# The last head's keys turned by DMA, its level products in pairs, an evacuation spread over chunks, and the front's modulation chunks four in a run

## The reference, cut to what matters

```
mod = silu(c) @ w_ada + b_ada;  shift, scale, gate = split(mod, 3)
h = rms_norm(x, norm_w) * (1 + scale) + shift
rq, rk, rv, rg, hq, hf_f, hf_b, hi, hg = split(h @ w_in, 9)
# HGRN2, in chunks: b = cumsum(log f)
scores = einsum(q, k, exp(b_i - b_j), causal)
o = scores @ v + (q * exp(b)) @ s
s = exp(b_last) * s + (k * exp(b_last - b)).T @ v
out = concat(o_r, o_h) @ w_out;  y = rms_norm(x + gate * out)
```

## Time and profile before

| | us |
|---|---|
| median of 3 runs | 1402.6 (1402.54 to 1402.9) |
| the profiled execution | 1402.41 |
| its span, first to last instruction | 1400.6 |
| TensorE busy | 1383.0 (99%) |
| VectorE busy | 1000.2 (71%) |
| ScalarE busy | 483.8 (35%) |
| GpSimd busy | 368.6 (26%) |
| mean granted TensorE clock | 0.999 of full |

### The profile page before, as it was taken

How to read it: one execution, slowest core, us unless ns; L and a number is a source line. 1 busy time by engine, 2 the same in 40 slices (tenths; PEclk the granted TensorE clock), 3 DMA queues, 4 the chain that set the end, 5 groups by cost and what they waited for, 6 DMA issues and landing times.

```text
span 1400.6 us, 24706 instructions
## 1 busy us (share of the span) xinstructions
PE 1383.0 (99%) x10042; PEld 1165.1 (83%) x10042; DVE 1000.2 (71%) x1330; ACT 483.8 (35%) x842; POOL 368.6 (26%) x292
## 2 busy tenths in 40 slices
PE   7999999999999999999999999999999999999997
PEld 5788898889888988898889888988898888888886
DVE  5555676667689888988888888877676768532345
ACT  4323243234333433342334333333333344221234
POOL 0000114311532153215321532153206225201220
PEclk9999999999999999999999999999999999999999
DMA  9994342434354535454444454433433358183235
GB/s 387 418 418 162 117 126 68 121 73 138 89 165 113 169 101 169 110 156 119 161 116 140 128 155 125 131 97 106 113 99 87 103 149 280 52 305 96 90 106 210
DMA packets 207735, 212.40 MB, mean 152 GB/s; under 512 B 144256, under 2 KB 156816, under 8 KB 202768
## 3 DMA queue, kind: packets, MB, share of 16 engines
q1 hardware_dynamic: 207600, 210.89, 48.0%
q10 hardware_dynamic: 32, 0.02, 0.0%
HBM read 182.27 MB, written 24.40 MB: 148 GB/s over the span
## 4 chain that ended last, share of the span: by engine, by line
PE 95%; DMA 3%; DVE 1%; SPq 0%; issue 0%; ACT 0%; DVEq 0%; ACTq 0%
PE ps L2133 10%; PE ps L2135 10%; PE ps L2134 10%; PE ps L1968 9%; PE ps L1969 8%; PE ps L1970 8%; PE ps L1944 8%; PE ps L2317 5%; PE ps L2319 5%; PE ps L2318 5%; DMA area<-in_w_mod 2%; PE ps L2150 2%; PE ps L1975 2%; PE ps L1976 2%; PE ps L1977 2%; PE ps L1934 2%
## 5 line engine op out<-in xcount | busy, mean ns | idle before, releaser
L1202 DVE TENSOR_TENSOR w_lo<-area,w_hi 128x1024 fp32r<-128x1024 f32 x143 | 190.4, 1331 | 206.3 <-ACT w_hi L730 206.3
L730 ACT ACTIVATE w_hi<-area 128x1024 fp32r<-128x1024 f32 x143 | 151.5, 1059 | 482.3 <-PE ps L2135 257.6
L2133 PE MATMUL ps<-w_hi,hT_hi 128*128 128x512 f32 x640 | 250.5, 391 | 0.0
L2135 PE MATMUL ps<-w_hi,hT_lo 128*128 128x512 f32 x640 | 249.1, 389 | 0.0
L2134 PE MATMUL ps<-w_lo,hT_hi 128*128 128x512 f32 x640 | 249.0, 389 | 0.0
L1968 PE MATMUL ps<-hT_hi,w_hi 128*128 128x512 f32 x512 | 204.8, 400 | 0.0
L1969 PE MATMUL ps<-hT_lo,w_hi 128*128 128x512 f32 x512 | 199.7, 390 | 0.0
L1970 PE MATMUL ps<-hT_hi,w_lo 128*128 128x512 f32 x512 | 199.6, 390 | 0.0
L2135 PEld LDWEIGHTS ps<-w_hi,hT_lo 128*128 128x128 f32 x640 | 120.1, 188 | 25.0
L2133 PEld LDWEIGHTS ps<-w_hi,hT_hi 128*128 128x128 f32 x640 | 120.2, 188 | 24.6
L2134 PEld LDWEIGHTS ps<-w_lo,hT_hi 128*128 128x128 f32 x640 | 120.2, 188 | 24.6
(11 more groups left out here) (282 smaller groups left out, 2426.5 us busy)
## 6 DMA issues: line engine op xcount, KB each, us to landing
area<-in_w_in SPq DMA_DIRECT2D x144, 512.0 KB, 4.3
area<-in_w_mod SPq DMA_DIRECT2D x26, 1024.0 KB, 12.3
area<-in_w_out SPq DMA_DIRECT2D x38, 512.0 KB, 3.8
gate_raw<-in_w_gate SPq DMA_DIRECT2D x32, 512.0 KB, 3.8
gate_raw<-in_w_mod SPq DMA_DIRECT2D x6, 1024.0 KB, 12.1
o_hi_scratch<-area SPq DMA_DIRECT2D x56, 80.0 KB, 2.4
o_lo_scratch<-area SPq DMA_DIRECT2D x56, 80.0 KB, 2.4
hT_hi<-o_hi_scratch SPq DMA_DIRECT2D x14, 320.0 KB, 7.2
```

What stands on the lines that cost most here:

```text
L730: act.activation(split_weights(h, n)[0], raw[:, n % 3, :], ACT.Copy).then_inc(wt_hi.sem, 1)
L1202: v.tensor_tensor(lo, raw[:, n % 3, :], hi.bitcast(F32), ALU.subtract).then_inc(wt_lo.sem, 1)
L2133: mm(out, hT_hi[:, k, tile_cols(t)], w_hi[:, n % 2, w], start=k == 0, stop=False)
L2135: i = mm(out, hT_lo[:, k, tile_cols(t)], w_hi[:, n % 2, w], start=False, stop=k == KT - 1)
```

## The change

It has four parts. (1) The last head's keys go the way of the other heads: `turn_keys` on DVE, `move_keys` on SP (behind `load_w_out(2)`); PE's eight transposes and ACT's two copies go, and `chunk_updates` waits for the DMA. (2) On PE, levels 4 and 5 of the last head's products stand together behind `first_block(3, 1)`, and 6 and 7 together behind `first_block(5, 0)`; products 5 and 7 get banks of their own; `place(4)` and `place(6)` now wait until both products of their pair are done. On DVE, `own_decay(5)` moves behind `differences(6)` and `place(6)` behind `own_decay(6)`. (3) In the last output block, DVE's evacuation of tiles 2, 3 and 4 is spread over three chunks. (4) In the front's four periods from e = 3 on, all four modulation chunks run together behind `first_group(e, 0)` and the queries.

```diff
 def ctx_scores(following, product):
     if following is None:
-        return ps[:, BB if product <= 2 else DD, 0:P]
+        return ps[:, BB if product <= 2 else DD, 0:P] if product not in (5, 7) else ps[:, DD, P:2 * P]
 def scores_bank(following, product):
-    return C if following is not None and product in (5, 7) else A
+    return C if product in (5, 7) else A
@@ sync
     load_w_out(2)
+    move_keys(last)
     store_states(last, n_ret_f, n_ret_b, rst, r_state, r_state_stored)
@@ scalar: keys() and its call go
     decays(last, 2)
-    keys(last)
     split_w(2)
@@ vector
 def place(h, following, product):
-    scored, placed = pe_level.at(h, (product if following is None else product | 1) + 1), h_sT.at(h, product)
+    scored = pe_level.at(h, (product if following is None and product < 4 else product | 1) + 1)
+    placed = h_sT.at(h, product)
...
     tokens_last(h)
-    if not isinstance(h, int) or h < HEADS - 1:
-        turn_keys(h)
+    turn_keys(h)
...
     place(last, None, 4)
     differences(last, 5)
-    own_decay(last, 5)
     place(last, None, 5)
     differences(last, 6)
-    place(last, None, 6)
+    own_decay(last, 5)
     split_w(5)
     own_decay(last, 6)
+    place(last, None, 6)
     hgrn_silu(last, 2)
     split_w(6)
     hgrn_silu(last, 3)
     place(last, None, 7)
...
+    late = nb == OUT_BLOCKS - 1
     if j == 2:
-        finish(nb - 1, 2, TILES)
+        finish(nb - 1, 2, 3 if late else TILES)
+    if late and j in (3, 4):
+        finish(nb - 1, j, j + 1)
@@ tensor
 for e in range(3, WCHUNKS - 1):
-    c0 = (e + 1) * GROUP_CHUNKS
-    ada_chunk(c0)
-    ada_chunk(c0 + 1)
     first_group(e, 0)
     first_queries(0, range(e + 1, e + 2))
-    ada_chunk(c0 + 2)
-    ada_chunk(c0 + 3)
+    for c_ in range((e + 1) * GROUP_CHUNKS, (e + 2) * GROUP_CHUNKS):
+        ada_chunk(c_)
     first_group(e, 1, range(0, 1))
...
 def chunk_updates(h):
-    if h == HEADS - 1:
-        pe.wait_ge(last_keys.sem, last_keys.at(0))
-    else:
-        pe.wait_ge(k_moved.sem, k_moved.at(h))
-        pe.wait_ge(r_S.sem, r_S.at(h))
-        pe.wait_ge(r_state.sem, r_state.at(h))
+    pe.wait_ge(k_moved.sem, k_moved.at(h))
+    pe.wait_ge(r_S.sem, r_S.at(h))
+    pe.wait_ge(r_state.sem, r_state.at(h))
...
-    if following is None or product in (2, 4, 6):
+    if product in (2, 4, 6) or following is None and product in (1, 3):
         pe.wait_ge(h_sT.sem, h_sT.at(h, product))
...
-    pe.wait_ge(r_scaled.sem, r_scaled.at(last))
-    key_tokens(last)
     pe.wait_ge(h_sT.sem, h_sT.at(last, 3))
     for kk in range(WK):
         first_block(0, kk, shared)
+    pe.wait_ge(r_scaled.sem, r_scaled.at(last))
     chunk_updates(last)
...
     first_block(3, 0)
+    first_block(3, 1)
     level_scores(last, None, 4)
-    first_block(3, 1)
     level_scores(last, None, 5)
     first_block(4, 0)
-    level_scores(last, None, 6)
     first_block(4, 1)
     first_block(5, 0)
+    level_scores(last, None, 6)
     level_scores(last, None, 7)
     first_block(5, 1)
     hgrn_outputs(last)
```

More of the change, by code:

```diff
@@ L325, in layer @@
         h_sq, h_rms, h_gated = Signal("h_sq"), Signal("h_rms", 2), Signal("h_gated")
-        last_keys, pe_hu, pe_level = Signal("last_keys", 2), Signal("pe_hu"), Signal("pe_level", PRODUCTS)
+        pe_hu, pe_level = Signal("pe_hu"), Signal("pe_level", PRODUCTS)
         pe_ho = Signal("pe_ho")
@@ L858, in retention_norm @@
                 i.then_inc(r_scaled.sem, 1)
[L860 to L864, removed]
             def context_states(h):
@@ L2201, in retention_columns, with chunk_updates @@
                 nc.tensor.transpose(ctx_columns(following), sT[:, 0:P], ident).then_inc(pe_columns.sem, 1)
-            def key_tokens(h):
-                pe.wait_ge(h_kl.sem, h_kl.at(h))
+            def chunk_updates(h):
+                pe.wait_ge(k_moved.sem, k_moved.at(h))
                 pe.wait_ge(r_S.sem, r_S.at(h))
                 pe.wait_ge(r_state.sem, r_state.at(h))
[L2208 to L2214, removed]
-                if h == HEADS - 1:
-                    pe.wait_ge(last_keys.sem, last_keys.at(0))
-                else:
-                    pe.wait_ge(k_moved.sem, k_moved.at(h))
-                    pe.wait_ge(r_S.sem, r_S.at(h))
-                    pe.wait_ge(r_state.sem, r_state.at(h))
                 for i, t in enumerate((0, 1, 2, 3)):
```

## The result

The kernel after takes 1406.67 us (median of 8 runs, 1406.02 to 1408.48), the kernel before 1402.65 (8 runs, 1402.33 to 1403.91) on the same chip: a ratio of 1.0029, 95% interval 1.0020 to 1.0038. That is slower by 4.0 us, where +1.6 was predicted, and outside the range of 1401.8 to 1406.2. The profiled execution of after took 1407.79 us, so it is one of the longer ones; its span grew by 5.4 us, from 1400.6 to 1406.0.

The account below looks back on a forecast made before the run. TensorE, busy for 99% of the span, was taken to bound the kernel. The terms -0.2 - 0.9 + 1.4 + 0.2 - 0.6 + 2.3 - 0.6 gave +1.6 us, median 1402.6 to 1404.2, range 1401.8 to 1406.2.

Parts of the forecast that it names:

- Levels 4 and 5: Last head: VectorE waits about 4 us at place(4), but three half blocks (10 us) precede level 6, so no cost.
- `place(7)`, +2.3: Last head: TensorE waits at hgrn_outputs for VectorE's place(7), delayed by work queued behind place(6); +2.3 us, bounds 2.0 and 2.6.
- Two pairs, -0.6: Last head's level products: running levels in pairs saves one pair of run ends, 0.28 us each, -0.6 us for two.
- -0.9, +1.4 and +0.2: Last head's keys: transposes gone -0.9 us; TensorE waits for VectorE's late retention_chain +1.4; follow-up at split_w(2) and state chain +0.2.
- Front, -0.2: Front's four periods: runs of four chunks save 1.28 us, waits for the low half cost 0.5 + 3 x 0.2; -0.2 us.
- The upper bound: Front: +0.5 us if each restart costs twice the forecast amount.
- Evacuations, -0.6: Last output block: the 0.34 us wait for a split behind three evacuated tiles goes, with overlap and restart; -0.6 us.
- the rivals: VectorE keeps up, 1399.2 us (6%); keys come late, 1407.2 (7%); front's slots run dry, 1406.2 to 1407.4 (10%).
- "Slower": Whole kernel: a time above 1405.4 us, from the two slow rivals and the forecast's edge; 19%.
- the keys or the slots: Slow rivals: last head's keys landing 3 us late, 1407.2 us (7%); front's chunk refills late, 1406.2 to 1407.4 us (10%).

Follow-up runs that it names:

- e1: The kernel before with only the paired level products (TensorE's and VectorE's order, two new buffers); 1407.06 us.
- e3: The kernel after with VectorE's hgrn_silu(2) moved ahead of own_decay(6) and place(7) put directly behind place(6); 1403.83 us.
- e4: The kernel after with levels 6 and 7 apart again, TensorE's order, banks and waits as before for them; 1404.88 us.
- e8: The kernel of e3 with levels 4 and 5 apart again as before, 6 and 7 still paired; 1402.24 us.
- e12: The kernel before with three reciprocals and a 32-column copy, read by nobody, added on VectorE ahead of hgrn_silu(3); 1407.96 us.
- e13: The kernel of e8 with the last head's keys on TensorE and the front as before; 1401.28 us.
- e6: The kernel before with only the spread evacuations of the last output block; 1401.61 us.
- e2: The kernel before with only the last head's keys turned by VectorE and moved by DMA; 1403.29 us.
- e5: The kernel before with only the front's run of four modulation chunks; 1402.34 us.
- e11: The kernel before with two reciprocals and a 128-column copy, read by nobody, added on VectorE ahead of hgrn_silu(3); 1404.59 us.
- e9: The kernel of e7 with SP's queue reordered: o loads ahead of move_keys, state stores and load_w_out(3) between its write and reads; 1403.70 us.
- e10: The kernel of e8 with the keys turned behind retention_chain and SP's order as in e9; 1402.76 us.
- e7: The kernel of e2 with VectorE's turn_keys moved behind retention_chain; 1404.20 us.

## Why the prediction was wrong

By medians the parts alone give +0.2 (front), +1.0 (keys), -0.6 (evacuations), and the pairs +3.3 without and about +4.8 with the fall of the clock. Without it the sum is +3.8 (unrounded); the five shorter runs of after lie 3.7 over before (1406.37 to 1402.65), the three longer ones 5.1 or more. So the parts add up. Of the miss of 2.4 us, 1.6 lie in the pairs (+3.3, where -0.6 + 2.3 was forecast), and what is left in the keys (0.3) and the front (0.4), each of them within the noise.

- *"Levels 4 and 5: VectorE waits about 4 us at `place(4)`, but three half blocks (10 us) follow before level 6. Nothing."* This step failed. It held VectorE's wait against TensorE's next product and stopped there. It did not ask what VectorE hands on behind `place(4)`, namely `differences(5)`, without which ScalarE's `decays(5)` and then GpSimd's `key_decay(5)` cannot start, nor did it name GpSimd's own `differences(5)`, for which the end of product 4 frees a buffer. Put off by 3.2 us, the chain for levels 5 and 6 (differences, exponentials, products) ends after TensorE has come to level 7. It showed as 1.1 us ahead of level 7 (after, e1, e3), as 2.3 ahead of level 6 when that was moved up (e4), and as nothing when product 4 went back (e8).
- *`place(7)`, +2.3.* Right in place, releaser and nearly in size: 2.09. e3 confirms the reason: it came from three operations of VectorE queued between `place(6)` and `place(7)`, and it goes when one of them is put into the idle time ahead (2.66 us before `own_decay(6)` in after) and the two others behind `place(7)`.
- *The price of a wait.* The sum took a wait as its length and now and then 0.11 us. It missed that behind a long one TensorE may run at its lower level for some 3 us. The profiled runs of after and e12 show it, at 1.6 us each; going by the times, it was there in three of after's eight runs, four of e1's five, four of e4's ten and all of e12's. The term is not in the list of waits; it is in the granted clock of the stretch.
- *Two pairs, -0.6.* A pair gives 0.3 when it runs in one piece: 0.97 us in e8, and e13 lies 0.4 below e6. In after levels 6 and 7 were torn apart, so this was half gone, and in e1 `hgrn_outputs` came exactly the two waits later than before, 3.2 us, with no saving left to see.
- *Keys.* -0.9, +1.4 and +0.2 were forecast; they measured +1.0 in all (e2, e13), with the wait at 1.42 in after and the round trip covered: `chunk_updates` had no wait. The mechanism is right. One bound was reasoned rightly as well: GpSimd's keys took 2.96 us with VectorE at rest beside them, 3.56 in the earlier trace rows.
- *Front, -0.2.* Measured at +0.2, not to be told from nothing (e5). The mechanism is right: in e5's trace a run of four takes 3.63 us up to the next wide matmul (74.19 to 77.82) for 3.64, the wait at e = 3 is 0.4, and at e = 4 TensorE is 0.2 us late (81.67 for 81.48), as forecast. The slots did not run dry. The upper bound was summed wrongly: restarts at twice their price give 2 x 1.1 - 1.28 = +0.9 and not +0.5.
- *Evacuations, -0.6.* Right by the medians: -0.6 in e6, with an interval that takes in no change, and no wait in TensorE's 30 us from 1335 on.

Of the rivals none came true. "Slower" had 19%, mostly by way of the keys or the slots; the way that it took had no chance of its own.

## What to carry to other kernels

When a product is moved back in TensorE's program, list every engine that waits for it, those too to whom it only frees a buffer, and follow each of them through what it hands on next, until the chain comes back to TensorE. A wait that has time to spare for the step in which it stands can hold up the step behind it. A pair saved 0.3 us here, and holding back its first half cost 1.1. Where two operations are paired for one consumer, put that consumer's other queued work ahead of the wait or behind the pair's results: that alone gave 2.5 us. And count a wait of TensorE of 2 us and more as possibly 1.6 us longer than it is.

## What the runs showed of the hardware

- Behind a wait the granted clock fell to the lower level (1.2 GHz) not at once but 0.6 us (e12) to 1.2 us (after) after TensorE had begun again, and came back some 3.4 us later; 1.6 us were lost in both. With a last-head wait of 1.4 or 1.5 us (e2, e3, e8, e11) none of 44 runs lies 1.4 us above the median of its kernel. With 2.1 to 2.3 us (after, e1, e4) 11 of 23 form a group 1.4 to 1.7 us above the rest, and with 3.4 us (e12) all 5 are as long as with a fall. This sorting goes by the times and is not sharp: of 101 runs of the kernel before, beside the experiments, 12 lie 0.8 to 1.4 us above their median without any such wait. In the window from 1215 us the clock is 0.66 in the profiled runs of after and e12 and 1.00 in the others. The Trainium skill (TensorE: Matmul & The Clock Gate, Why this matters for your kernels) warns of idle gaps between bursts for this reason, but of longer ones than the 2.1 us that was enough here.
- Falls as long stand in the front of six profiled runs, with 0.78 to 0.88 in the windows of 5 us: from 5 to 15 us in after, e1, e9 and e10, from 25 to 35 us in e12 and e13. The latter two had waited 1.65 and 1.74 us for a chunk of `w_mod` just before; e3, e4 and e7 waited 1.7 us at the same place and had no fall. So the length of the one wait does not decide by itself, and what does is open. A mean clock over the whole run does not tell where a fall stood.
- GpSimd's 128x320 differences took 0.71 us with VectorE idle (after, 1204.02) and 1.70 beside VectorE's split at 1202.36, a subtraction with two inputs, and that split took 2.03 instead of some 1.2. The Trainium skill (GPSIMD Engine Reference, Key points) says that the two share their way to SBUF for such operands; the trace agrees. Over levels 5 and 6 this cost GpSimd's chain nothing on balance: it met VectorE elsewhere before, and took 9.2 us there and 9.1 here.
- A round trip of 512 KB through DRAM had its write and its first read 5.5 us apart at 1160 us (after) and 2.6 us apart at 1165 (e7), so a length read off one head was no measure for another moment.
